# A decoder layer on one core: index, query and key tiles in three passes of rounded parts, the convolution's running sums in PSUM

## The reference

```python
mod = silu(c) @ w_ada + b_ada                        # six vectors per sequence
h   = rms_norm(x, g1) * (1 + scale1) + shift1
q, k, v, qi, ki, wi, u_conv, gates = split(h @ w_in)  # one projection, columns partitioned
q, k = rms_norm(q, g_q), rms_norm(k, g_k)             # per head of 128
I[t,s] = sum_h wi[t,h] * relu(qi[t,h] . ki[s])        # picks the top-k causal keys
attn   = softmax(q . k - alibi) v   over the picked keys
z = a * sigmoid(g)  (a, g = halves of u_conv)
y = causal depthwise convolution of z, width 31, + b_dw; then LayerNorm, swish, w_conv_out
merged = sigmoid(gA) * (attn @ w_o) + sigmoid(gB) * conv_out ;  x += gate1 * (merged @ w_out)
x += gate2 * peer(h2)     # 128 x 128 experts by product keys, top 16 per head; 8 heads
```

## Time and profile before

| | |
|---|---|
| median of 3 executions | 1273.83 us (1270.83 to 1274.44) |
| the profiled execution, its own time | 1271.0 us |
| its span in the trace | 1269.2 us |
| PE busy | 1223.2 us, 96% |
| DVE, ACT, POOL busy | 921.1, 572.3, 535.8 us |
| mean granted clock of TensorE | 0.991 of full speed |

### The profile page before, as it was taken

How to read it: one execution, slowest core, us unless ns; L and a number is a source line. 1 busy time by engine, 2 the same in 40 slices (tenths; PEclk the granted TensorE clock), 3 DMA queues, 4 the chain that set the end, 5 groups by cost and what they waited for, 6 DMA issues and landing times.

```text
span 1269.2 us, 27591 instructions
## 1 busy us (share of the span) xinstructions
PE 1223.2 (96%) x8591; PEld 1108.0 (87%) x8591; DVE 921.1 (73%) x2246; ACT 572.3 (45%) x992; POOL 535.8 (42%) x272
## 2 busy tenths in 40 slices
PE   5999999998998999999999999999999999999998
PEld 3777677987987999999999999999888888888886
DVE  4499955876644999959999999100467888888866
ACT  2200134655544444645555555444454545545543
POOL 1100015430655567676666666777402434433100
PEclk9999999899997999999999999999999999999999
DMA  9875455354453346665555555667767898888863
GB/s 357 315 253 200 152 191 199 120 162 134 152 171 113 128 167 212 191 208 178 186 181 181 186 177 187 197 209 239 255 238 273 299 342 310 302 299 304 281 228 130
DMA packets 113993, 273.09 MB, mean 215 GB/s; under 512 B 30928, under 2 KB 54192, under 8 KB 113552
## 3 DMA queue, kind: packets, MB, share of 16 engines
q1 hardware_dynamic: 98752, 243.71, 56.4%
q0 software_dynamic: 6432, 19.71, 4.6%
q10 hardware_dynamic: 8752, 8.93, 2.2%
HBM read 249.30 MB, written 23.00 MB: 215 GB/s over the span
## 4 chain that ended last, share of the span: by engine, by line
PE 91%; DVE 2%; DMA 2%; ACT 1%; issue 1%; SPq 1%; ACTq 0%; POOL 0%; DVEq 0%; POOLq 0%
PE ps L2123 19%; PE ps L2073 10%; PE ps L2066 10%; PE ps L2067 10%; PE ps L2126 10%; PE ps L1713 9%; PE ps L1755 5%; PE ps L1763 5%; PE ps L1769 4%; PE ps L2102 2%; DMA ring<-in_stream 1%; PE ps L1785 1%; PE ps L1845 1%; PE ps L2043 1%; DMA s_act_dram<-act 1%
## 5 line engine op out<-in xcount | busy, mean ns | idle before, releaser
L675 POOL TENSOR_TENSOR split<-ring,split 128x1024 fp32r<-128x1024 f32 x128 | 307.2, 2401 | 142.4 <-ACT split L982 142.4
L982 ACT ACTIVATE split<-ring 128x1024 fp32r<-128x1024 f32 x256 | 271.5, 1061 | 174.4 <-PE ps L2123 169.7
L2066 PE MATMUL ps<-h2r,split 128*128 128x288 f32 x1024 | 278.7, 297 | 3.1 <-ACT split L982 3.1
L2067 PE MATMUL ps<-h2r,split 128*128 128x288 f32 x1024 | 278.9, 296 | 0.0
L2123 PE MATMUL ps<-h2r,split 128*128 128x512 f32 x1024 | 257.4, 392 | 1.4 <-DVE h2r L1602 1.4
L2123 PEld LDWEIGHTS ps<-h2r,split 128*128 128x128 f32 x1024 | 184.2, 189 | 34.5 <-ACT act L1011 1.6
L2066 PEld LDWEIGHTS ps<-h2r,split 128*128 128x128 f32 x1024 | 192.9, 188 | 3.6 <-ACT split L982 1.9
L2067 PEld LDWEIGHTS ps<-h2r,split 128*128 128x128 f32 x1024 | 192.4, 188 | 0.0
L640 POOL TENSOR_TENSOR split<-ring,split 128x1024 fp32r<-128x1024 f32 x48 | 118.6, 2473 | 155.8 <-ACT split L773 155.8
L2073 PE MATMUL ps<-h2r,split 128*128 128x288 f32 x1024 | 156.8, 295 | 0.3
L1608 DVE TENSOR_TENSOR split<-ring,split 128x1024 fp32r<-128x1024 f32 x128 | 155.9, 1218 | 0.0
(11 more groups left out here) (278 smaller groups left out, 1592.8 us busy)
## 6 DMA issues: line engine op xcount, KB each, us to landing
ring<-in_stream SPq DMA_DIRECT2D x379, 512.0 KB, 3.4
act_dram<-act SPq DMA_DIRECT2D x128, 128.0 KB, 1.7
parts<-act_dram SPq DMA_DIRECT2D x16, 512.0 KB, 4.6
big<-act_dram SPq DMA_DIRECT2D x16, 512.0 KB, 5.2
big<-in_stream SPq DMA_DIRECT2D x12, 512.0 KB, 11.2
big<-in_cache_k ACTq DMA_DIRECT2D x16, 128.0 KB, 3.5
big<-in_cache_v ACTq DMA_DIRECT2D x16, 128.0 KB, 3.5
s_act_dram<-act SPq DMA_DIRECT2D x128, 16.0 KB, 1.4
```

The lines of the kernel that those rows point to most:

```text
L675: nc.gpsimd.tensor_tensor(split[:, n % 2, 1], ring[:, slot_of(n), :], split[:, n % 2, 0].bitcast(f32), ALU.subtract).then_inc(lo_ready, 1)
L982: nc.scalar.activation(split[:, n % 2, 0], ring[:, slot_of(n), :], ACT.Copy).then_inc(hi_ready, 1)
L2066: MM(out, u_hi[:, k], h_hi[:, k], start=(k == 0), stop=False)
L2067: last = MM(out, u_hi[:, k], h_lo[:, k], start=False, stop=False)
```

## The change

The five index tiles and the ten key and query tiles join the first stage of `CUT`, so they go through `linear_cut`; conv_a and conv_g stay in `linear`. `NHEAD` is the index of gate_a0 in the new list, 15. ACT cuts a tile at the key of HEAD whose load position is one before it, ahead of what else it does at that key. POOL makes the low parts of the first 13 head tiles, then the two stores of the state, then the other two. DVE's running sums of a pair lie in the bank pa[3] (`conv_ps`), only the last tap writes y in SBUF; the next pair's gated inputs are made ahead of tap 15 (of 0 to 30) of the pair before; conv_a tiles use three banks and wait for z three chunks back; for the sample windows the weights are first copied to the same bank (`wdw_ps`).

```diff
--- before.py
+++ after.py
@@ -158,8 +158,11 @@
         n_evac += 2
         ACT_EVAC[key] = n_evac
 
-STAGES = [("gate_a", "gate_b"), ("conv_out",), ("attn_out",), ("out",), ("peer_q",)]
+STAGES = [("ki", "qi", "k", "q", "gate_a", "gate_b"), ("conv_out",), ("attn_out",), ("out",), ("peer_q",)]
 CUT = [key for key in PLAN if any(key[0] in kinds for kinds in STAGES)]
+
+NHEAD = CUT.index(("gate_a", 0))
+KEY_AT = {POS[key]: key for key in CUT}
 QK = [("k", n) for n in range(KV)] + [("q", n) for n in range(H)]
 QK_AT = 3
 
@@ -381,6 +384,9 @@
         ps = [ctx.enter_context(nc.psum_tensor(f"ps{b}", [P, 512], f32)) for b in range(8)]
         lin, adab, stb, pa = ps[0:NBANK], ps[2], ps[3], ps[4:8]
         iota_ps = ps[7][:, 0:P]
+
+        conv_ps = pa[3][:, :].rearrange("p (k t) -> p k t", t=TP)
+        wdw_ps = pa[3][:, 0:KC * CW].rearrange("p (k j) -> p k j", j=CW)
 
         place_ps = [adab[:, t * 2 * P:(t + 1) * 2 * P].rearrange("p (w k) -> p w k", w=2) for t in range(NQ)]
         place_ps.append(pa[3][:, 0:2 * TS].rearrange("p (w k) -> p w k", w=2))
@@ -625,21 +631,29 @@
             nc.gpsimd.tensor_tensor(rhs_parts[:, 1], hT[:, :, :].rearrange("p k t -> p (k t)"),
                                     rhs_parts[:, 0].bitcast(f32), ALU.subtract).then_inc(rhs_lo, KC)
 
+            def low_tile(n):
+
+                pool.wait_ge(lin_hi, n + 1)
+                if n >= 2:
+
+                    pool.wait_ge(tile_done, POS[CUT[n - 2]] + 1)
+                nc.gpsimd.tensor_tensor(split[:, n % 2, 1], ring[:, POS[CUT[n]] % R, :], split[:, n % 2, 0].bitcast(f32),
+                                        ALU.subtract).then_inc(lin_lo, 1)
+
+            def low_tiles(kinds):
+
+                for n, key in enumerate(CUT):
+                    if key[0] in kinds:
+                        low_tile(n)
+
+            for n in range(NHEAD - 2):
+                low_tile(n)
+
             pool.wait_ge(conv_staged, 2)
             pool.dma_start(a["convpT"], staged_p).then_inc(conv_stored, 16)
             pool.dma_start(a["convsT"], staged_s).then_inc(conv_stored, 16)
-
-            def low_tiles(kinds):
-
-                for n, key in enumerate(CUT):
-                    if key[0] in kinds:
-                        pool.wait_ge(lin_hi, n + 1)
-                        if n >= 2:
-
-                            pool.wait_ge(tile_done, POS[CUT[n - 2]] + 1)
-                        nc.gpsimd.tensor_tensor(split[:, n % 2, 1], ring[:, POS[key] % R, :],
-                                                split[:, n % 2, 0].bitcast(f32), ALU.subtract).then_inc(lin_lo, 1)
-
+            for n in range(NHEAD - 2, NHEAD):
+                low_tile(n)
             low_tiles(("gate_a",))
             pool.wait_ge(y_prompt, KC)
             pool.wait_ge(y_sample, 1)
@@ -790,6 +804,8 @@
 
             for key in HEAD:
                 kind, m = key[:2]
+                if kind not in ("v", "turn") and POS[key] + 1 in KEY_AT:
+                    cut_tile(KEY_AT[POS[key] + 1])
                 if kind == "conv_a":
                     continue
                 if kind == "ada":
@@ -815,8 +831,6 @@
                         .then_inc(act_evac, 1)
                 else:
                     n = QK.index(key)
-                    if n == len(QK) - 1:
-                        cut_tile(("gate_a", 0))
                     evac(key, kT[:, m] if kind == "k" else q[:, m])
                     evac(key, sq_qk[n], ACT.Square)
                     if key == ("q", 3):
@@ -839,7 +853,7 @@
                     root(3)
                 if n % 2 == 0:
                     if n:
-                        cut_tile(CUT[n // 2 + 1])
+                        cut_tile(CUT[NHEAD + n // 2 + 1])
                     evac(("gate_a", n // 2), ga[:, n // 2], ACT.Sigmoid)
                     key = GATE_A[GATE_A.index(("gate_a", n // 2)) + 1]
                     if key[0] == "turn":
@@ -867,7 +881,7 @@
 
             eng.wait_ge(qk_ready, KV)
             for n in range(KC):
-                cut_tile(CUT[KC + n + 1])
+                cut_tile(CUT[NHEAD + KC + n + 1])
                 if n == 0:
 
                     for k in range(KC):
@@ -1126,24 +1140,33 @@
             dve.wait_ge(conv_in, 64)
             dve.wait_ge(state_in, 1)
             dve.wait_ge(zeroed, 6)
-            for pair in range(KC // 2):
+            def gated_input(pair):
                 for k in (2 * pair, 2 * pair + 1):
                     dve.wait_ge(tile_done, POS["conv_a", k] + 1)
                     dve.wait_ge(sig_ready, k + 1)
-                    V.tensor_tensor(zp[:, k, LEFT:], pa[k % 4][:, 0:TP], sig[:, k, 0:TP], ALU.mult)\
+                    V.tensor_tensor(zp[:, k, LEFT:], pa[k % 3][:, 0:TP], sig[:, k, 0:TP], ALU.mult)\
                         .then_inc(z_ready, 1)
-                    V.tensor_tensor(zs[:, k, :, LEFT:], seq(pa[k % 4][:, TP:T]), seq(sig[:, k, TP:T]), ALU.mult)\
+                    V.tensor_tensor(zs[:, k, :, LEFT:], seq(pa[k % 3][:, TP:T]), seq(sig[:, k, TP:T]), ALU.mult)\
                         .then_inc(z_ready, 1)
+
+
+            gated_input(0)
+            for pair in range(KC // 2):
                 dve.wait_ge(z_ready, 4 * pair + 4)
+                if pair:
+                    dve.wait_ge(y_prompt, 2 * pair)
                 for j in range(CW):
+                    if j == CW // 2 and pair + 1 < KC // 2:
+                        gated_input(pair + 1)
                     for k in (2 * pair, 2 * pair + 1):
-                        yp, w = y[:, k, 0:TP], wdw[:, k, j:j + 1]
+                        acc, w = conv_ps[:, k % 2], wdw[:, k, j:j + 1]
                         if j == 0:
-                            ins = V.tensor_scalar(yp, zp[:, k, 0:TP], w, cvec[:, 0, k:k + 1], ALU.mult, ALU.add)
+                            ins = V.tensor_scalar(acc, zp[:, k, 0:TP], w, cvec[:, 0, k:k + 1], ALU.mult, ALU.add)
                         else:
 
                             settle(1 if j < CW - 1 or k % 2 == 0 else 0)
-                            ins = V.scalar_tensor_tensor(yp, zp[:, k, j:j + TP], w, yp, ALU.mult, ALU.add)
+                            ins = V.scalar_tensor_tensor(acc if j < CW - 1 else y[:, k, 0:TP], zp[:, k, j:j + TP], w, acc,
+                                                         ALU.mult, ALU.add)
                         if j < CW - 1:
                             step(ins)
                         else:
@@ -1151,10 +1174,12 @@
 
 
             samples = y[:, :, TP:T].rearrange("p k (b t) -> p k b t", t=TD)
+            dve.wait_ge(y_prompt, KC)
+            step(V.tensor_copy(wdw_ps, wdw))
             for t in range(TD):
                 settle()
                 step(V.tensor_tensor(windows, zs[:, :, :, t:t + CW],
-                                     wdw.unsqueeze(2).to_broadcast([P, KC, NSEQ, CW]), ALU.mult))
+                                     wdw_ps.unsqueeze(2).to_broadcast([P, KC, NSEQ, CW]), ALU.mult))
                 settle()
                 step(V.tensor_reduce(samples[:, :, :, t], windows, AX.X, ALU.add))
             settle()
@@ -1697,10 +1722,10 @@
             def linear(key, rhs, chunk_ready=None):
 
                 if key[0] == "conv_a":
-                    bank = pa[key[1] % 4]
-                    if key[1] >= 4:
-
-                        pe.wait_ge(z_ready, 2 * (key[1] - 4) + 2)
+                    bank = pa[key[1] % 3]
+                    if key[1] >= 3:
+
+                        pe.wait_ge(z_ready, 2 * (key[1] - 3) + 2)
                 else:
                     bank = lin[BANK[key]]
                     free(BANKED.index(key))
@@ -1845,8 +1870,10 @@
                         last = MM(lin[n % NBANK][0:rows, 0:VW], hT[:, k, cols], v_w[:, k], start=(k == 0),
                                   stop=(k == KC - 1))
                     last.then_inc(v_done, 1)
+                elif key[0] in ("conv_a", "conv_g"):
+                    linear(key, hT, h_ready if key == ("conv_a", 0) else None)
                 else:
-                    linear(key, hT, h_ready if key == ("conv_a", 0) else None)
+                    linear_cut(key)
                     if key in QK[1:]:
                         qk_sum(QK.index(key) - 1)
```

## The result

| | before | after |
|---|---|---|
| median | 1274.0 us (6 runs, 1270.83 to 1274.96) | 1281.43 us (6 runs, 1279.62 to 1283.77) |
| ratio, 95% interval | | 1.0062 [1.0048, 1.0077] |
| the profiled execution and its span | 1271.0, 1269.2 us | 1283.77, 1282.0 us |
| mean granted clock | 0.991 | 0.982 |

A forecast was written before the change was run, and what follows sets the result against it. PE, busy 96% of the span, was taken as the bound. Saving 10.3 us against 14.8 of waits gave +4.5, plus 2.3 for the clock +6.8: 1281 us on the median, range 1273 to 1287.

The forecast's parts named there:

- Saved by rounding: PE in the head: 15 index, key and query tiles go from 4.07 to 3.38 us, saving 10.3 us.
- Waits for ACT: PE waits for ACT's late cuts before eight head tiles; with POOL's late parts and 1.7 back, 14.8 us.
- The clock: PE's clock falls to the lower level after the idle before ki: +2.3 us, bounds 0 and 4.6.
- a second time before q4: Rival of a second or longer clock fall, such as at q4's wait: +2.3 to +4.8 us more; chance 0.12.
- The sum: Whole kernel: +4.5 us from waits against savings, plus 2.3 for the clock, makes +6.8 us.
- DVE: Some 13 us standstill in pair 2, taps no slower; 4.4 us of cover left before the reciprocal, so no cost.
- What follows the head shifts as a whole.: From gate_a on, everything moves later together, with no extra cost counted.
- Faster, cuts early: Rival: page transfers and evacuations do not delay ACT's cuts, ki starts near 81, no tile waits: 1265 us; chance 0.07.
- Port: Rival: taps' pointer scalar counts as second SBUF input, so POOL's subtractions hold DVE: +19 us, 1300; chance 0.04.

The follow-up runs named there:

- e2: Changed kernel with conv_g5's page transfers behind qi3's evacuation and every head cut ahead of the preceding matmul tile's evacuation: 1262.07 us, ratio 0.9915.
- e1: Changed kernel with conv_g5's page transfers issued behind qi3's evacuation instead of ahead of ki: 1272.7 us, ratio 1.0008.
- e11: Changed kernel with ACT's two copies of the convolution's state behind q4's evacuation instead of q3's: 1279.37 us, ratio 1.0043.
- e10: Changed kernel with 12 useless float32 matmuls filling PE's idle time ahead of ki: 1278.17 us, ratio 1.0035.
- e12: Changed kernel with the next pair's gated inputs made ahead of tap 27 instead of 15: 1281.09 us, ratio 1.0063.
- e4: Kernel before with only the PSUM sums and window weights, three conv_a banks and mid-pair gating; tiles stay float32: 1274.86 us, ratio 1.0015.
- e9: e2 with the mean that centres y left in PSUM and gated inputs made ahead of tap 27: 1261.39 us, ratio 0.9902.
- e7: Changed kernel with the mean that centres y left in PSUM: 1279.94 us, ratio 1.0052.
- e3: Changed kernel with the running sums and window weights back in SBUF: 1324.39 us, ratio 1.0397.
- e6: Kernel before with the mean that centres y left in PSUM: 1274.12 us, ratio 1.0002.

## Why the prediction was right

Forecast 1281.0, measured 1281.43; +6.8 forecast, +7.4 measured. By its steps:

- **Saved by rounding.** A first tile of a pair takes 3.53 to 3.66 with POOL's part late, a second 3.28 to 3.39: about as costed (3.58 and 3.38). The price of a float32 tile, 4.07, holds where something else follows it; two in a row took 7.96 in the kernel before (91.41 to 99.37), and five of the fifteen stood like that, which makes the saving some 0.5 smaller. e2, in which nothing is late, shows the sum: its head is 12.4 us shorter than the kernel before's (87.90 against 100.30), of which 1.8 are the wait before qi0, so the fifteen tiles gave 10.6 where 10.3 was forecast.
- **Waits for ACT.** Forecast 6.9, 1.0, 1.0, 0.9, 0.7, 0.9, 2.8, 0.7 before ki, qi1, qi3, k0, q0, q2, q4, q6. Measured 6.78, 0.96, 0.96, 1.07, 0.81, 0.75, 2.83, 0.82. None before the other seven. e1 and e11 each took one cause away, and its wait went.
- **The clock.** Forecast 2.3 before ki, measured 1.5 (e10): the slow stretch lasted 4.1 us from ki's start, not 5.7. The clock also fell a second time before q4, 1.2 us, which the prediction had only as a rival: 1.5 + 1.2 = 2.7 together, where 2.3 was in the sum. This term came out because two errors nearly cancelled.
- **The sum.** In the two profiled executions the head is +8.05, not +6.8. The difference is made of the 0.4 of the clock, the 0.5 of the float32 pairs and about 0.5 for the overlap of 0.08 us between neighbouring matmuls, which is lost at each wait, less some 0.3 by which three second tiles were cheaper than costed. The medians' +7.4 holds the head and whatever the gate_a stretch adds in a typical execution, which the forecast put at nothing. That it lies within 0.6 of the forecast is therefore partly luck.
- **DVE.** Forecast waits of 13 us for two sigmoids and 4.4 left before the reciprocal; measured 12.8 and 5.10. Taps in PSUM 0.393 apart. e12 and e4 show it as cover from both sides.
- **"What follows the head shifts as a whole."** This step failed in the profile: the gate_a stretch grew 3.0 us. It is the one thing that the prediction costed at nothing without naming what could meet there. 1.5 of it is DVE held by POOL in the centring of y (e9 and e7); the slow rows behind are open. In the medians no more than about 1.5 of it is seen (e7).
- **Rivals.** *Faster, cuts early* named the right place and the right condition; e1 and e2 made it true, and the time was 1262.1 against the 1265 of the rival. It had left out the wait before qi0 and let DVE's slack allow 9 us of what PE gained; the head became 12.4 shorter and DVE held PE for only 1.08 of it. *Port* was refuted for the changed kernel: taps with one SBUF tensor, PSUM and a pointer were never held by POOL (28 in 11.06 us, none over 492 ns). It is not refuted for every operation with a pointer scalar, as e3's first taps, one SBUF tensor and two pointers with the result in SBUF, took 2.2 to 2.5 us each beside POOL. And where two tensors came from SBUF its account of the loss was wrong: it had DVE wait for POOL and DVE's slack pay for it; in e3 DVE's loss was covered, and the 43 us came from POOL starving with PE behind it.

## What to carry to other kernels

When work moves from a matmul engine to a helper's hand-off, the hand-off's place in the helper's program costs more than its rate: go through the helper's instructions one by one up to the new one, the transfers that it issues included, and put the new one ahead of everything that waits for the tile before. Eight transfers that nobody needed soon decided here between 7.4 us slower and level, and the order of the rest between level and 12 us faster. And if VectorE and GpSimd read SBUF beside each other, keep a long back-to-back stream to one SBUF input: here its accumulator and the window weights in PSUM cost 0.5 to 3.3 us by themselves (e4) and were worth 43 us beside GpSimd's subtractions (e3).

## What the runs showed that was not expected

- A GpSimd subtraction of 2.4 us that began beside VectorE's back-to-back taps with two SBUF inputs took 7.88, 10.35 and 22.17 us: it did not get in between two VectorE instructions 0.4 us apart, for as long as their row went on, while those taps lost nothing. With GpSimd in first, VectorE waited (4.69 for 2.56; single taps of 1.73 and 2.61).
- Idle times of 2.83, 2.85, 2.72, 2.68 and 1.97 us on PE, each in a stretch of otherwise dense matmuls, were followed, at once or within 4 us, by some two rows of eight matmuls at about 2 us instead of 1.2. The length of the idle does not settle it: an idle of 1.38 us at the same place was followed by such rows in e4 and not in the kernel before, e1, e2, e6, e7 or e9. Waits of 0.75 to 1.07 in the head never were, nor was the 1.74 before qi0. Behind the sample scores, 64 small matmuls after an idle of 0.74, such rows stand in every profile (the earlier trace rows at 232.58).
